# The second layer's scores: a low-order pass on 64 rows, two key groups on the two halves of the partitions

## What is computed

```python
q = _apply_axial_rope(_diff_heads(q), cos, sin)          # 8 heads, 2 maps, 1024 tokens, 64
k = _apply_axial_rope(_diff_heads(k), cos, sin)
k_all = jnp.concatenate([k, kc], axis=3)                 # 1024 + 256 keys
s = jnp.einsum('bhmqd,bhmkd->bhmqk', q, k) * scale       # scores
p = jax.nn.softmax(s, axis=-1)
a = p[:, :, 0] - lam * p[:, :, 1]
y = jnp.einsum('bhqk,bhkv->bhqv', a, v)
out = (rms_norm(y) * silu(z)) @ w_out
```

## Time and profile before

| | us |
|---|---|
| median of 3 executions | 1812.74 |
| lowest, highest | 1811.44, 1813.02 |
| the profiled execution: its time | 1811.31 |
| its profiled span | 1809.5 |
| PE matmul busy in the span | 1772.5 (98%) |
| DVE, ACT, POOL busy | 1253.1, 916.5, 290.1 |
| second layer's scores: 768 matmuls (L1767) | 176.8 |

### The profile page before, as it was taken

How to read it: one execution, slowest core, us unless ns; L and a number is a source line. 1 busy time by engine, 2 the same in 40 slices (tenths; PEclk the granted TensorE clock), 3 DMA queues, 4 the chain that set the end, 5 groups by cost and what they waited for, 6 DMA issues and landing times. The chain is left out here.

```text
span 1809.5 us, 30712 instructions
## 1 busy us (share of the span) xinstructions
PE 1772.5 (98%) x10461; PEld 1532.6 (85%) x10461; DVE 1253.1 (69%) x2236; ACT 916.5 (51%) x1648; POOL 290.1 (16%) x251
## 2 busy tenths in 40 slices
PE   7999999999999999989999999999999999999998
PEld 3898889898888888878878988888888888898886
DVE  6677777767676767765877576675848485757758
ACT  2555555555655556560046555564737465554500
POOL 3200000000000000355441010101000010102951
PEclk9999999999999999999999999999999999999999
DMA  9414141414132232335420010101010000001343
GB/s 348 114 50 109 47 108 49 110 38 105 55 97 63 80 79 63 97 96 186 166 82 24 13 46 12 46 0 46 12 41 17 35 23 24 34 12 46 101 146 128
DMA packets 82368, 133.31 MB, mean 74 GB/s; under 512 B 41825, under 2 KB 50177, under 8 KB 82193
## 3 DMA queue, kind: packets, MB, share of 16 engines
q1 hardware_dynamic: 68496, 106.48, 18.5%
q0 software_dynamic: 11088, 16.78, 4.1%
q10 hardware_dynamic: 2736, 9.44, 1.3%
HBM read 106.54 MB, written 17.73 MB: 69 GB/s over the span
## 5 line engine op out<-in xcount | busy, mean ns | idle before, releaser
L523 PE MATMUL acc<-h_hi,w_hi 128*128 128x512 f32 (+1 forms) x1408 | 523.6, 372 | 3.1 <-DVE h_lo L448 1.8
L523 PE MATMUL acc<-h_hi,w_lo 128*128 128x512 f32 (+1 forms) x1408 | 508.4, 361 | 0.0
L523 PE MATMUL acc<-h_lo,w_hi 128*128 128x512 f32 (+1 forms) x1408 | 507.9, 361 | 0.0
L523 PEld LDWEIGHTS acc<-h_hi,w_lo 128*128 128x128 f32 x1408 | 265.4, 188 | 41.3
L523 PEld LDWEIGHTS acc<-h_hi,w_hi 128*128 128x128 f32 x1408 | 265.8, 189 | 40.3 <-DVE h_lo L448 4.7
L523 PEld LDWEIGHTS acc<-h_lo,w_hi 128*128 128x128 f32 x1408 | 266.3, 189 | 33.6
L1660 DVE TENSOR_REDUCE stats<-acc 128x1 f32<-128x1280 f32 x128 | 189.7, 1487 | 43.6 <-PE acc L1767 42.9
L1570 ACT ACTIVATE far_prob<-acc,stats 128x1280 f32<-128x1280 f32 x128 | 170.1, 1329 | 28.3 <-DVE stats L1660 26.6
L1577 ACT ACTIVATE far_pt<-acc 128x512 f32<-128x512 f32 (+1 forms) x192 | 101.0, 526 | 162.5 <-PE acc L1776 159.0
L1767 PE MATMUL acc<-k_dup,q_stack 128*128 128x512 f32 (+1 forms) x768 | 176.8, 367 | 1.8 <-ACT far_prob L1570 0.4
L1789 PE MATMUL acc<-far_v,far_pt 128*128 128x128 f32 x1280 | 172.6, 275 | 0.0
(11 more groups left out here) (209 smaller groups left out, 2942.2 us busy)
## 6 DMA issues: line engine op xcount, KB each, us to landing
w_raw<-in_w_in SPq DMA_DIRECT2D x64, 512.0 KB, 3.3
near_late_slots<-in_w_mod SPq DMA_DIRECT2D x64, 256.0 KB, 2.7
w_raw<-in_w_out SPq DMA_DIRECT2D x16, 512.0 KB, 3.3
w_raw<-y_t POOLq DMA_DIRECT2D x14, 448.0 KB, 5.2
near_values<-near_values POOLq DMA_DIRECT2D x16, 384.0 KB, 4.3
y_t<-y SPq DMA_DIRECT2D x7, 640.0 KB, 3.0
modulation_rows<-in_w_scale SPq DMA_DIRECT2D x8, 512.0 KB, 6.4
modulation_rows<-in_w_mod SPq DMA_DIRECT2D x8, 512.0 KB, 6.4
```

Source lines behind the costliest of these rows:

```text
L523: mm = nc.tensor.matmul(m.bank(self.bank_of(j, c), w), wt[:, b % 2, k, :], ht[:, k, t0:t0 + w], start=(k == 0 and i == 0), stop=(k == KT - ...
```

## The change

The first pass of `scores` is as before: three matmuls (512, 512, 256 keys) on 128 rows against the high keys, now all three ahead of the second pass. The second pass no longer computes q_lo k_lo. It multiplies only high queries with low keys, on 64 rows: key groups 0 and 2 on the map's own half of the partitions, group 1 on the other half. For that the high queries are wanted on the other half too, in a new buffer `far_q_other` (128 partitions x 1024, fp32r): two more DVE copies of 64x512 per chunk behind the low queries of tokens 0 to 511, and two more ACT copies of 64x512 in `late_q_hi`, with a new semaphore `q_copied` for which PE waits at tiles 0 and 4.

```diff
@@ FarProjection
+    def q_other_of(self, h, g):
+        t0, w = GROUPS[g]
+        return self.far.q_other[64 - 64 * h:128 - 64 * h, t0:t0 + w]
+
@@ late_q_hi
             self.nc.scalar.activation(hi, y, ACT.Copy).then_inc(self.q_hi, 1)
+        for h in range(2):
+            hi, y = self.q_hi_of(h, 1)
+            self.nc.scalar.activation(self.q_other_of(h, 1), y, ACT.Copy).then_inc(self.q_copied, 1)
@@ dve_part
                 self.split_q_lo(v, self.nc.vector, c, 0)
+                for h in range(2):
+                    hi, y = self.q_hi_of(h, 0)
+                    self.nc.vector.tensor_copy(self.q_other_of(h, 0), y).then_inc(self.q_copied, 1)
@@ differential, scores(mp, t)
                         if mp == 0 and t in (0, 4):
                             pe.wait_ge(p.q_ready, CREDIT + c * 4 + (2 if t == 0 else 4))
+                            pe.wait_ge(p.q_copied, CREDIT + c * 4 + (2 if t == 0 else 4))
+                        queries = slice(t * P, (t + 1) * P)
                         for g, (k0, w) in enumerate(GROUPS):
-                            for part in range(2):
-                                mm = nc.tensor.matmul(m.bank(3 * mp + g, w), m.q_stack[:, mp, t * P:(t + 1) * P],
-                                                      m.k_dup[:, mp, part, k0:k0 + w], start=(part == 0), stop=(part == 1))
+                            nc.tensor.matmul(m.bank(3 * mp + g, w), m.q_stack[:, mp, queries], m.k_dup[:, mp, 0, k0:k0 + w],
+                                             start=True, stop=False)
+                        own, other = slice(64 * mp, 64 * mp + 64), slice(64 - 64 * mp, 128 - 64 * mp)
+                        for g, (k0, w) in enumerate(GROUPS):
+                            rows, q = (other, far.q_other[other, queries]) if g == 1 else (own, m.q_stack[own, mp, queries])
+                            mm = nc.tensor.matmul(m.bank(3 * mp + g, w), q, m.k_dup[rows, mp, 1, k0:k0 + w], start=False, stop=True)
                         mm.then_inc(s_done, 1)
```

More of the change, by code:

```diff
@@ L185, in __init__ @@
         self.pt = sb("pt", [P, 4, 512])
+        self.q_other = sb("q_other", [P, SEQ], F32R)
 def rows_broadcast(ap_row, n):
@@ L725, in __init__ @@
         self.k_own, self.q_ready, self.k_hi, self.q_hi = (self.sem(n) for n in ("k_own", "q_ready", "k_hi", "q_hi"))
+        self.q_copied = self.sem("q_copied")
         self.rot_shuffled, self.rot_scaled, self.dve = (self.sem("rot_" + n) for n in ("shuffled", "scaled", "dve"))
```

## The result

The changed kernel takes 1827.01 us (median; 1826.74 to 1827.89), the kernel before 1812.84 in the same comparison: a ratio of 1.0082 (95% interval 1.0070 to 1.0095), 14.2 us slower. Forecast were 1829.3, which is 16.6 us slower, in a range of 1804 to 1842. The executions of either kernel spread by more than 1 us; lowest against lowest the difference is 15.3.

The account below looks back on a forecast made before the run. PE was taken to bound the kernel, at 2.4 GHz. Per chunk 1.06 + 1.02 = 2.08 us, over 8 chunks 16.6, added to the 1812.74 median gave 1829.3 us, range 1804 to 1842.

Parts of the forecast that it names:

- 0.20 us for each change of shape: Into and out of the 64-row pass: array empties (0.09 us) and the next weight load lies open, 0.20 us each.
- Rival A: At the 64-row pass: changes of shape are free, each scores 0.23 us shorter, 1805 us in all; chance 0.14.
- rival B: At the shape changes: array empties, 0.09 us each, but weight loads stay hidden; 1815 us in all; chance 0.13.
- 0.34 us for the three groups on two halves: Second pass of a scores: group 1 streams beside group 0, group 2 behind group 0, 0.34 us instead of 0.57.
- C: Second pass: the halves run one after the other, or the change fails; 0.40 us more per scores, 1853 us; chance 0.13.
- The load of group 2: In the 64-row pass: hidden under a running matmul by the rows; by the skill's overlap rule open, 0.11 us more.
- D: In the 64-row pass: group 2's load stands open, 0.28 us more per scores, 1839 us in all; chance 0.08.
- d = 0.17: Growth of each scores: 0.20 + 0.34 + 0.20 = 0.74 us against 0.57, so 0.17 us more.
- scores(0) of the loop hidden, scores(1) in full: Tile loop: six map 0 scores' growth hidden by a 0.22 us exponential wait; map 1's six add 1.02 us per chunk.
- ACT's copies ahead of the first exponential: scores(0,1) 0.72 late: Chunk start: four ACT copies instead of two delay the first exponential, so scores(0,1) comes 0.72 us late.
- Tile 0 1.06 late, and six times d behind it: Per chunk: tile 0 starts 0.72 + 0.34 = 1.06 us late, map 1's six scores add 1.02; sum 2.08 us.
- Eight equal chunks: Whole second-layer loop: the 2.08 us per chunk counted for 8 chunks alike, 16.6 us.

Follow-up runs that it names:

- e7_six: Kernel before, with each key group's 128-row matmul followed by its 64-row one on the map's own half, six shape changes per scores: 1956.29 us.
- e4_own: Kernel before, with the new pass order and a 64-row second pass all on the map's own half, no copies: 1845.68 us.
- e6_map1: Kernel before, with the new scores only for map 1 in the tile loop and the copies made by GpSimd: 1821.70 us.
- e5_map0: Kernel before, with the new scores only for map 0 in the tile loop and the copies made by GpSimd: 1815.65 us.
- e2_copies: Changed kernel with its copies and waits kept, but the old six 128-row matmuls in each scores: 1821.24 us.
- e11: Kernel before, with GpSimd's output-weight split in the second layer cut from 1024 columns to 64, result incomplete: 1810.10 us.
- e12: Changed kernel, with GpSimd's output-weight split in the second layer cut from 1024 columns to 64, result incomplete: 1824.42 us.
- e10_act_later: Changed kernel, with ACT's two added copies moved behind the first exponentials, between exp(1,0) and exp(0,1): 1820.34 us.
- e9_pair: Kernel before, with scores(0,0) and scores(1,0) of each chunk sharing one 64-row stretch, each map on its own half, no copies: 1810.10 us.

## Why the prediction was right

The sign, the mechanism and the places held, and the size to 2.4 us. By the steps:

*PE sets the pace, at the clock's top.* Held in all that was changed: 98% and a mean granted clock of 0.998. The one fall inside the stages, at 776, lies ahead of it.

*0.20 us for each change of shape.* Held. The rows with 2 columns and with 32 rows, were a good measure for 64 rows: 0.09 empty and 0.11 of load at 1007.23 and at 1007.77, and 0.196 in the chunks of e7_six at the full clock. One of these rows was weaker than I made it: the load at 154.99 is marked as released by DVE's L374, which ran from 154.16 for 0.75, to 154.91, so its 0.09 need not be the array's. The other three places carry the reading. The Trainium skill's sentence in TensorEngine Tiling (Array Packing), section Tiling Modes, that changing the tiling mode drains the TensorE, agrees with these rows; the price is the rows'. Rival A (free) and rival B (loads hidden) are ruled out by e4_own, which gains nothing by overlap and loses 33 us.

*0.34 us for the three groups on two halves.* The sum held (0.11 + 0.227 for group 0, then group 2), its making did not: I let group 1's load come behind that of group 0, and in the trace the two loads and the two matmuls start 0.004 apart. It changes nothing, since group 2 behind group 0 sets the end. The Trainium skill, TensorEngine Tiling (Array Packing), section Key Properties, lets different tiles load weights and multiply in parallel, and these rows agree. C (one half after the other) falls with e4_own.

*The load of group 2.* By the rows it should be hidden, by the rule cited in the prediction open. It starts at 1007.34 beside the running matmuls, and group 2 follows group 0 at once: in this kernel the rule did not hold, and D (1839) falls. Here the measurement decides.

*d = 0.17.* Held: 0.16 per tile in tiles 2 to 5, and what map 1 adds in e6_map1.

*scores(0) of the loop hidden, scores(1) in full.* Held for map 0 (e5_map0 adds nothing in its loop) and for five of the six scores of map 1 (e6_map1), and the row shrank from 48 waits to 19.

*ACT's copies ahead of the first exponential: scores(0,1) 0.72 late.* Held: 0.74, and 0.73 in e2_copies.

*Tile 0 1.06 late, and six times d behind it.* This is the term that was too large: 2.08 per chunk against 1.73. scores(0,2), right behind tile 0, is 0.98 late, and over the next two tiles only 0.14 is added, to 1.12 at scores(0,4), where 0.34 was reckoned; the last four add 0.61 and not 0.68. In the kernel before, the first tiles wait longer for the exponential than the tile of the earlier trace rows: scores(1,3) starts 2.33 us behind scores(0,3), where the later pairs lie 2.24 apart, and in the changed kernel this pair too. So the cover was larger there, and growth of PE's work went into it. I had read the wait from one tile late in a chunk and used it for all six. That is 0.08 + 0.20 + 0.07 = 0.35 per chunk, 2.4 us in seven.

*Eight equal chunks.* They are seven and one. The last grew by 3.2 to its end, 1.1 more than the 2.08 of the sum: its start had less slack, and DVE met GpSimd in other tiles (e11, e12). I had read the start of one chunk and multiplied by 8. By the traces the sum is then 16.6 - 2.4 + 1.1 = 15.3, the two errors partly cancelling. The rest to the medians' 14.2 is the spread of single executions. That the two traces differ by just the 16.6 forecast is luck: 1.2 of it are the clock's.

*The parts do not add up.* The copies alone cost 0.88 per chunk (e2_copies), the scores with ACT's copies out of the way 1.14 (e10_act_later), together 1.73 and not 2.02: PE's own 2d at the start lies inside the wait for the exponential, as the prediction had it. How much of e10's 1.14 is DVE's two copies was not tried.

## What to carry to other kernels

Count the changes of the array's shape before the columns saved: each costs 0.20 us, nearly a 512-column matmul (0.227), so the 0.23 saved by working on both halves is less than the two changes around it. A copy that is needed only tiles later still delays what everything waits for if it stands ahead of it in its engine's queue; put it behind. Read the wait that is to hide some work in the first, a middle and the last turn of a loop, not in one of them.

## What was not expected of the hardware

- Two 64-row loads on the two halves of the partitions start together (0.003 us apart), and so do their matmuls (0.004).
- The load for a 64-row tile hides under a matmul that runs on the same rows, just as with 128 rows: it starts at 1007.34, and its matmul 0.335 behind the one before, which is 0.11 of load and 0.227 of streaming of that one.
- Narrow passes of two different scores join without a break: in e9_pair the six matmuls of two maps, on opposite halves, share one stretch, 0.79 us from its first row to that of the next pass.
- GpSimd slows DVE. Beside GpSimd's 64x512 multiplication DVE's 64x512 cast took 0.79 us in the mean instead of 0.42 and the subtraction 1.05 instead of 0.69; a 128x1024 subtraction took 2.10 instead of 1.22 (and where it did not, the copy took 2.1 instead of 1.04), and the combine of 1280 columns 2.53 instead of 1.55.
- The clock's fall is hidden in a row of digits: 3.4 us at half of it cost 1.2 us of an execution and still showed as a 9 in its slice. In e7_six the six falls at the chunks' starts cost about 12 us.
